# Order of work inside the first attention of a long float32 kernel: turned-block copies, projection steps, splits, rotation and modulation sums placed at other units

## The reference, cut to what matters

```python
mod = cond @ ada_w[i] + ada_b[i]                     # 1024 x 6144, for the six vectors of a layer
proj = h @ w_in                                      # 1024 -> 512 (q) + 256 (kv) + 32 (k_rope)
q  = (rms_norm(q_lat, q_norm) @ w_qb).reshape(B, S, 16, 96)
q_rope = apply_rope(q[..., 64:], pos)                # 32 of 96 channels are rotated
kv = (rms_norm(kv_lat, kv_norm) @ w_kvb).reshape(B, S, 16, 128)
s = (q_nope @ k_nope + q_rope @ k_rope) * 96 ** -0.5 # causal, softmax over the keys
o = softmax(s) @ v
```

## Time and profile before

| | us |
|---|---|
| median of three runs | 3063.3 |
| the three runs | 3062.71, 3063.3, 3073.83 |
| span of the profiled execution | 3070.7 |
| the attention loop in it, from the first scores to the last values (124.42 to 315.48) | 191.1 |
| PE busy over the span | 2858.4 |
| DVE busy over the span | 1724.5 |
| ACT busy over the span | 1245.4 |

### The profile page before, as it was taken

One profiled execution on the slowest core, in us unless ns is written; L12 is line 12 of the kernel. 1 busy time (PEld: TensorE's weight loads), 2 busy tenths in 40 slices (PEclk: granted clock), 3 DMA queues, 4 the chain that ended last, 5 costly groups with the idle time before them and its releaser, 6 DMA issues. The chain is left out here.

```text
span 3070.7 us, 40665 instructions
## 1 busy us (share of the span) xinstructions
PE 2858.4 (93%) x16535; PEld 2438.6 (79%) x16535; DVE 1724.5 (56%) x2989; ACT 1245.4 (41%) x2250; POOL 248.9 (8%) x224
## 2 busy tenths in 40 slices
PE   5988899999997989889999999899999998899998
PEld 4766787787886879789999997688788866678886
DVE  5666554435774866443468887543425386654344
ACT  3455432223433343323467776432223345432222
POOL 0000000000002452010000001112100002200000
PEclk7899999999999999889999999999999999999999
DMA  5222234422231111053479997211231203412321
GB/s 220 76 108 102 96 144 171 157 103 96 83 144 55 56 42 56 27 204 120 170 262 353 344 339 275 76 62 46 91 122 45 83 32 121 157 69 81 113 85 65
DMA packets 74418, 387.94 MB, mean 126 GB/s; under 512 B 8490, under 2 KB 10190, under 8 KB 42574
## 3 DMA queue, kind: packets, MB, share of 16 engines
q1 hardware_dynamic: 60816, 349.20, 31.2%
q10 hardware_dynamic: 10382, 26.07, 2.4%
q0 software_dynamic: 3024, 9.98, 0.9%
HBM read 368.43 MB, written 22.03 MB: 127 GB/s over the span
## 5 line engine op out<-in xcount | busy, mean ns | idle before, releaser
L342 DVE TENSOR_TENSOR wlo<-stage,whi 128x1024 fp32r<-128x1024 f32 (+4 forms) x524 | 533.7, 1059 | 350.8 <-ACT whi L354 350.1
L354 ACT ACTIVATE whi<-stage 128x1024 fp32r<-128x1024 f32 (+4 forms) x524 | 443.8, 896 | 211.2 <-PE ps L638 171.0
L638 PE MATMUL ps<-whi,mxhi 128*128 128x256 f32 x968 | 282.7, 292 | 13.3 <-DVE wlo L342 9.0
L638 PE MATMUL ps<-whi,mxlo 128*128 128x256 f32 x968 | 275.5, 285 | 0.0
L638 PE MATMUL ps<-wlo,mxhi 128*128 128x256 f32 x968 | 275.3, 284 | 0.0
L638 PE MATMUL ps<-bxhi,whi 128*128 128x512 f32 x480 | 200.9, 419 | 17.1 <-DVE bxlo L342 8.4
L638 PEld LDWEIGHTS ps<-whi,mxhi 128*128 128x128 f32 x968 | 186.7, 193 | 16.4 <-DVE wlo L342 6.2
L638 PE MATMUL ps<-bxhi,wlo 128*128 128x512 f32 x480 | 190.0, 396 | 0.0
L638 PE MATMUL ps<-bxlo,whi 128*128 128x512 f32 x480 | 189.7, 395 | 0.0
L638 PEld LDWEIGHTS ps<-wlo,mxhi 128*128 128x128 f32 x968 | 187.2, 193 | 0.0
L638 PEld LDWEIGHTS ps<-whi,mxlo 128*128 128x128 f32 x968 | 187.0, 193 | 0.0
(11 more groups left out here) (591 smaller groups left out, 6573.0 us busy)
## 6 DMA issues: line engine op xcount, KB each, us to landing
stage<-in_gu SPq DMA_DIRECT2D x91, 1024.0 KB, 6.7
more<-in_gu SPq DMA_DIRECT2D x41, 1024.0 KB, 6.7
stage<-in_ada SPq DMA_DIRECT2D x40, 1024.0 KB, 4.9
stage<-in_dn SPq DMA_DIRECT2D x36, 768.0 KB, 5.4
stage<-in_dn SPq DMA_DIRECT2D x32, 640.0 KB, 4.3
stage<-in_gin SPq DMA_DIRECT2D x16, 1024.0 KB, 4.8
stage<-in_gt SPq DMA_DIRECT2D x16, 1024.0 KB, 4.7
more<-in_dn SPq DMA_DIRECT2D x16, 640.0 KB, 4.6
```

The lines of the kernel that those rows point to most:

```text
L342: return e.do.tensor_tensor(out, x, y, op)
L354: return e.do.activation(out, x, f, **kw)
L638: return self.p.do.matmul(out, lhsT, rhs, start=start, stop=stop, skip_group_check=True)
```

## The change

All of it is in the first attention. The computation is the same; the order of instructions on PE, ACT and DVE and the order of the loads differ.

- ACT's turned copy(n - 3) stands ahead of exponential(n) instead of behind it.
- The ten projection steps of a group stand at units 6, 7, 0, 1, 2 (q: 2, 2, 2, 1, 1 steps) and 4 (k: 2 steps), between turn(n - 3) and values(n - 4). Only the first group keeps 3, 3, 2 steps at n = 0, 1, 2 and 2 at n = 4.
- ACT's `queries` moved behind the output copy of unit 3; `keys` from unit 4, ahead of the turned copy, to unit 5, behind the output copy.
- The splits: those of k stay at unit 2, but on ACT behind the output copy; those of q go from unit 7 (two halves) to units 4 and 6 (one half each).
- DVE's rotation: two multiplications at unit 3 (`turn`), one addition each at units 4 and 5 (`join`).
- A modulation piece takes three visits of three and two instructions at units 7, 0, 1, 2, 4 and 5, the first at n = 7; none at units 3 and 6. `pe_ada` follows one step behind the end of a piece, at units 2 and 6.
- The loads: two modulation pieces behind each q piece, then the k piece.

```diff
-    for g in range(8):
-        w("wq", [g])
-        if 1 < g < 7:
-            c(1)
+    w("wq", [0])
+    w("wk0", [0])
+    w("wq", [1])
+    for g in range(1, 8):
         w(f"wk{g}", [0])
...
         if g < 7:
-            c(1)
+            w("wq", [g + 1])
+            c(2)
...
+    def mla_steps(self, n):
+        if n < 6:
+            return (3, 3, 2, 0, 2, 0)[n]
+        return (2, 1, 1, 0, 2, 0, 2, 2)[n % 8] if n < 53 else 0
+    def mla_ada(self):
+        return [n for n in range(7, 54) if n % 8 in (7, 0, 1, 2, 4, 5)]
...
-            if n % 8 == 0 and n < 56:
-                more = self.mla_project(L, n // 8 + 1)
-            step = more if n % 8 and n < 64 else iter(())
+            if n == 0 or (n % 8 == 6 and n < 48):
+                more = self.mla_project(L, (n + 10) // 8)
             if n < 64:
                 scores(n)
-            next(step, None)
             if 3 <= n < 67:
                 turn(n - 3)
-            next(step, None)
+            for _ in range(self.mla_steps(n)):
+                next(more, None)
             if n > 3:
                 values(n - 4)
-            next(step, None)
...
+            if at == 2 and g < 8:
+                self.act_ahead(f"wk{g}", 0, False)
+            if at == 3 and g < 8:
+                queries(g)
+            if at in (4, 6) and g < 7:
+                self.act_ahead("wq", g + 1, False, 1)
+            if at == 5 and g < 8:
+                keys(g)
```

More of the change, by code:

```diff
@@ L889, in mla_pe @@
         units = self.mla_units()
-        more = None
+        more, done = None, self.mla_ada()[2::3]
         def scores(n):
@@ L1013, in mla_act @@
         keys(0)
+        self.act_ahead("wq", 1, False)
         for n in range(64 + 4):
-            g = n // 8 + 1
-            if n < 64:
-                w = (units[n][1] + 1) * P
-                c, sl = L.cols[n % 6], L.sl[n % 5]
-                a.wait_ge(V(("nm", n)))
-                act(a, sl[:, 0:w], sl[:, 0:w], ACT.Exp, bias=c[:, 5:6], scale=L.scale, accum_out=c[:, 4:5]).then_inc(*A.up(("e", n)))
-            if n % 8 == 2 and g < 8:
-                self.act_ahead("wq", g, False)
-                self.act_ahead(f"wk{g}", 0, False)
-            if n % 8 == 4 and g < 8:
-                keys(g)
+            g, at = n // 8 + 1, n % 8
             if 3 <= n < 67:
@@ L1032, in mla_act @@
                 act(a, L.pt[u % 4][:, 0:w], self.bank(("t", u))[:, 0:w], ACT.Copy).then_inc(*A.up(free(("t", u))))
-            if n % 8 == 3 and g < 8:
-                queries(g)
+            if n < 64:
+                w = (units[n][1] + 1) * P
+                c, sl = L.cols[n % 6], L.sl[n % 5]
+                a.wait_ge(V(("nm", n)))
+                act(a, sl[:, 0:w], sl[:, 0:w], ACT.Exp, bias=c[:, 5:6], scale=L.scale, accum_out=c[:, 4:5]).then_inc(*A.up(("e", n)))
             if n > 3:
@@ L1129, in mla_dve, with turn @@
             v.do.tensor_copy(L.k[k][64:96, :], L.kr[64:96, :]).then_inc(*V.up("turned"))
-        def queries(g):
+        def turn(g):
             use, r, r2 = (("q", g), 2 * g + 1), L.tmp[0], L.tmp[1]
@@ L1135, in queries, with join @@
             tt(v, r[0:64, :], b[0:64, :], cos[0:64, :], MUL).then_inc(*V.up())
-            tt(v, r2[0:64, :], b[64:128, :], sin[64:128, :], MUL).then_inc(*V.up(free(use)))
-            v.wait_ge(V.now())
+            tt(v, r2[0:64, :], b[64:128, :], sin[64:128, :], MUL).then_inc(*V.up(("qr", g), free(use)))
+        def join(g, h):
+            r, r2, s = L.tmp[0], L.tmp[1], slice(32 * h, 32 * h + 32)
+            v.wait_ge(V(("qr", g)))
             if g >= 2:
                 v.wait_ge(P_(("s", 8 * (g - 2) + 7)))
-            for h in range(2):
-                s = slice(32 * h, 32 * h + 32)
-                tt(v, L.q[(2 * g + h) % 4][64:96, :], r[s, :], r2[s, :], ADD).then_inc(*V.up(("qe", 2 * g + h)))
+            tt(v, L.q[(2 * g + h) % 4][64:96, :], r[s, :], r2[s, :], ADD).then_inc(*V.up(("qe", 2 * g + h)))
         units = self.mla_units()
         self.dve_ahead("wq", 0)
-        queries(0)
+        turn(0)
+        for h in range(2):
+            join(0, h)
         self.dve_ahead("wk0", 0)
+        self.dve_ahead("wq", 1, False)
         v.wait_ge(self.Dt[0]("tab"))
+        beats = self.mla_ada()
         def modulation():
             for n in range(8, 20):
-                yield from self.dve_ada(0, n)
+                yield from self.dve_ada(0, n, (3, 5) if n % 2 else (3, 6))
                 if n % 4 == 0 and n > 8:
@@ L1179, in mla_dve @@
                 v.do.reciprocal(c[:, 6:7], c[:, 4:5]).then_inc(*V.up(("rl", n - 4)))
-            if n % 8 == 7 and g < 7:
-                self.dve_ahead("wq", g + 1, False)
-            if n > 1:
+            if at == 2 and g < 8:
+                self.dve_ahead(f"wk{g}", 0, False)
+            if at == 3 and g < 8:
+                turn(g)
+            if at in (4, 5) and g < 8:
+                join(g, at - 4)
+            if at in (4, 6) and g < 7:
+                self.dve_ahead("wq", g + 1, False, 1)
+            if n in beats:
                 next(more, None)
```

22 lines of the change are left out of this document (6 added, 16 removed).

## The result

The changed kernel takes 3072.7 us (median of 12 runs, 3065.3 to 3083.3); beside it on the same chip the kernel before took 3065.7 (12 runs, 3058.7 to 3073.8). The ratio is **1.0023, 95% interval 1.0012 to 1.0033**: 7 us slower, within the 0.5% that was called no change. Forecast was 3083, clearly on the slow side. The measured time lies in the range, but the forecast gave a loss two to three times as large. The profiled execution of after has a span of 3076.3 us, 5.6 above that of before.

The account below looks back on a forecast made before the run. PE, busy 93% of the span, was taken as the bound, losing time only to waits and the slow clock. 3070.7 less 11.7 gained at full clock plus 24.6 for six clock falls gave 3083 us; range 3040 to 3097.

Parts of the forecast that it names:

- The round at full clock: Attention loop, from the end of the values of unit 2: 24.4 us a round, against 24.1 to 24.3 before.
- The list of PE's work: PE's matmul work in one round of the attention loop, added up to 18.7 us as the floor.
- e: Instant at which the values of unit 2 end; the laid-out round counts its times from there.
- The two stalls: PE idle at two hand-overs of bank 5 each round: 2.75 us for copies of q, 2.85 for copies of k.
- The first stretch and the tail: Before the five rounds, e at 153.05 instead of 157.5, gain 4.4 us; tail (n > 50), gain 2 us.
- The price of the clock: Clock falls to 0.50 in every round: six slow stretches at 4.1 us each, 24.6 us lost.
- Mean clock under 0.85 in most rounds: Profile sign, over the rounds of the attention loop, that the prediction is right.
- The base: Sum starts from 3070.7 us, without subtracting the 7.4 us by which the profiled span lies above the median.
- Loads: Modulation pieces loaded in pairs: DVE may wait 1 us at unit 7; costed at nothing, up to 3 us a round.
- The rivals: Other outcomes: clock holds 0.13, PE bound only by its work 0.20, DVE in time 0.14, worse 0.05; main course 0.48.
- Rival 2: ACT and DVE run ahead, both stalls under 1 us, clock up, rounds 19.5 to 21.5 us: 3036 us; chance 0.20.
- Rival 1: Same stalls in the loop but the clock holds: 3059 us, up to 3065 with one or two falls; chance 0.13.

Follow-up runs that it names:

- experiment 4: Changed kernel with only ACT's split of k at unit 2 put first in its step; 3056.6 us, ratio 0.9979 to the kernel before.
- experiment 2: Changed kernel with ACT's copies of q (unit 3) and k (unit 5) first in their step; 3059.4 us, ratio 0.9978 to the kernel before.
- experiment 5: Changed kernel with 14 extra unread matmuls ahead of the k steps of unit 4 and q steps of unit 6; 3064.5 us, ratio 0.9992.
- 3: Changed kernel with ACT's copies of q and k and all its splits first in their step; 3042.9 us, ratio 0.9929 to the kernel before.
- experiment 8: Kernel of 3 with PE's sum of a modulation piece two steps behind the piece's end instead of one; 3034.7 us, ratio 0.9917.
- experiment 6: Changed kernel with one part undone: projection steps back at units 1 to 4, 3075.9 us (1.0042); or turned copy back behind the exponential, 3078.4 us (1.0049).
- experiment 7: Kernel before with the turned copy ahead, plus the rotation spread, 3051.6 us (0.9958); or instead ACT's splits at units 2 and 7 first, 3054.7 us (0.9978).
- 1: Kernel before with only ACT's turned copy(n - 3) moved ahead of exponential(n); 3039.3 us, ratio 0.9914.
- the rotation: Kernel before with the turned copy ahead and DVE's rotation spread over units 3, 4 and 5; 3051.6 us, ratio 0.9958.

## Why the prediction was right in its course and wrong in its size

- **The round at full clock: right.** Laid out at 24.4, measured at 24.7 where the clock was kept up. (The list of PE's work adds up to 18.9 us, not 18.7, and the instants to 24.5; neither matters to the sum.) Even single instants hold: from e at 187.85 (the row start and 0.67) the copies of q were due at 192.1 and came at 192.08; PE's k step at 193.35 and came at 193.33. The second k-to-q step was due at 200.1 and came at 201.51, 1.1 of it because the steps behind the first stall ran at 1.2 GHz (195.84 less 193.33 is 2.5 us, where 1.4 stood).
- **The two stalls: right.** 2.75 and 2.85 were expected, 2.56 and 2.42 measured in that round, averages of 2.1 and 1.7 over seven. The second is shorter than laid out where the work ahead of it ran at 1.2 GHz and PE came late; at full clock it is 2.80 (experiment 4). That the copies stand too far back in ACT's list is shown by 2, and that the late split of k makes 0.9 us of the first stall by 4. How much of the second is the split of q, and how much the piece of the sum, was read from the trace and not tested alone.
- **The first stretch and the tail.** The tail gained 1.9 (2 expected). The first gained 2.6, not 4.4; the clock fell there once.
- **The price of the clock: the term that was mis-sized.** It was 6 falls of 4.1 us, taken from the dearest round of the earlier trace rows. But that price belongs to a length, not to a fall. The time at 1.2 GHz in a round is twice its length by one less the mean clock. In the earlier trace rows: 28.20 us at 0.76 is 13.5 us low for 4.1 us lost, 26.65 at 0.81 is 10.1 for 2.5, which is 0.3 and 0.25 us lost for each low one. In after, over 24.4:

| round, us | clock | low, us | lost, us | lost per low us |
|---|---|---|---|---|
| 33.02 | 0.64 | 23.8 | 8.6 | 0.36 |
| 25.94 | 0.93 | 3.6 | 1.5 | 0.42 |
| 28.00 | 0.82 | 10.1 | 3.6 | 0.36 |
| 26.96 | 0.87 | 7.0 | 2.6 | 0.37 |
| 26.64 | 0.87 | 6.9 | 2.2 | 0.32 |

  The clock did fall in every round, as forecast, but in four of the five it stood low for 4 to 10 us and not for the 13.5 that the price assumed; why it came back so soon was not found. Experiment 4 goes further: with 1.68 and 2.80 us of idling in a round the clock held in three rounds of five, so two long stalls don't bring it down each time. In all 18.5 us for five rounds and 1.8 for the first, 20.3 where 24.6 stood: 4.3 too much. In the loop the sum then comes out: 11.7 gained and 20.3 lost is 8.6 us more, and 8.8 were measured. "Mean clock under 0.85 in most rounds", given as a sign of being right, came true in two of five.
- **The base: the step that failed most.** The sum was made against the profiled span of 3070.7 and its distance of 7.4 us to the median was not subtracted, on a guess about the luck of the quick runs. It wasn't luck: beside the changed kernel, twelve runs of the kernel before had a median of 3065.7, 5.0 below that span. So 5.0 of the 10.3 us by which the forecast was too high are this base, 4.3 are the clock. A good part of the 5 us is seen behind the loop, in a stretch from the first `qkv` to the first `mxhi` that the change doesn't touch; before, after, and the kernel of experiment 4:

```profile
783.90:1313.60 529.70, 476.25 (x2942) 418.87 (x2941) 345.95 (x599) 205.49 (x424) 120.28 (x105) 0.95 0.19 69
```

```profile
793.30:1317.80 524.50, 471.13 (x2940) 414.08 (x2940) 346.12 (x599) 205.48 (x424) 120.32 (x105) 0.95 0.19 70
```

```profile
774.10:1307.10 533.00, 476.40 (x2941) 418.65 (x2940) 346.23 (x599) 205.25 (x423) 120.28 (x105) 0.94 0.19 69
```

  The same work took 529.7 us in the profiled execution of before, 524.5 in that of after, 533.0 in those of experiments 4 and 5, and 524.7 to 527.1 in the ten others. So this stretch swings by up to 8.5 us from one execution to another, whatever the loop ahead of it is, and the excess of before is no property of the code around the loop. The profiled runs of experiments 4 and 5 lie 5.0 and 5.5 us above the medians of their kernels, as the profiled span of before lies 5.0 above the median of twelve (6.3 like for like, since a run's span is 1.3 us below its time); that of after lies 4.9 above its median with this stretch short, so the excess can sit elsewhere too. No second profile of before was taken. With the sum's own difference (12.9) on the median, the forecast would have been 3078.6; with the clock's 4.3 less, 3074.3, against 3072.7 measured.
- **Loads: right at nothing.** DVE waited for a modulation piece twice in the loop, 1.0 us in all. The wait is there once the loop is quicker: 8.7 us in experiment 2 and 12.7 in 3.
- **The rivals.** None took place. Rival 2 asked what happens when ACT and DVE come in time: 20.5 a round was said, and experiment 8 shows 20.6 to 20.8 (19.1 in the first) once three orders are mended. Rival 1 (3059 with the clock held) has its likeness in experiment 5, 3064.5.

Where the gain of 26 us went is then settled in its main lines: the turned copy moved ahead saves 2.1 us a round, and the rest of the change puts two stalls of up to 2.6 in its place because ACT's splits and hand-overs stand behind an output copy that waits for PE. The parts don't add up, though: undoing one by one gave 1.0042 and 1.0049, mending the order in ACT's list 0.9979 and 0.9978 for one piece each and 0.9929 for both. The spread of the projection steps alone isn't the cause either: with them back (experiment 6) nothing was gained. Open is how much of each of these is the work in the list and how much the clock that followed.

## What to carry to other kernels

- In an engine that works in order, ask of each instruction that others wait for what stands ahead of it and what that waits for. An output copy that nobody needs soon, put ahead of a split or a hand-over, hands PE's lateness on to DVE and back to PE. Moving four such pieces ahead of it, and PE's sum one step later, was worth 32 us here (1.0023 to 0.9917), on a kernel whose engine work stayed the same.
- Price a low clock by its length (0.25 to 0.42 us for each microsecond at 1.2 GHz in this loop), not by the fall, and give the fall itself a chance and not a certainty: the same stalls brought it in some rounds and not in others.
- Before you put a split at the head of a step, look whether its weights have landed. In an engine that works in order, the wait for the load is handed to all that stands behind it; in experiment 7 the kernel with such splits was 20 us slower than without.
- Compare with the median. Here the profiled run lay 7.4 us above the median of three runs, and 5.0 above that of twelve; added to a forecast, this was its largest error.

## What the runs showed of the hardware

- **The clock fell behind idle stretches of 1.5 us, and held through one of 2.8.** At one place of the round, in the runs of 1 and of the rotation, it fell behind each of five stretches of 1.53 to 1.64 us and behind none of five of 0.90 to 1.41. In the run of experiment 4 two stretches of 1.68 and 2.80 us stand in each round, and it held in three rounds of five. Two stretches of 0.81 and 0.87 us, the second ending 2.7 us after the first, had 17 us at 1.2 GHz behind them in the run of 8. Before, 1.67 us brought no fall. So the length of one idle stretch doesn't decide it alone.
- **Work that nobody needs can pay.** 154 extra matmuls in the stalls made the changed kernel 9 us faster (experiment 5).
- **PE can be busy for long at the low clock.** In the run with the turned copy back in 8, PE was busy 33.0 of 34 us at a mean clock of 0.50, the longest low stretch seen; in that of experiment 2, 30.5 of 31 us at 0.51.
- **The same work doesn't take the same time.** A stretch of 524.5 us in one profiled execution took 533.0 in two others whose code in it is the same.
